# Hybrid attention and mLSTM layer: four kinds of TensorE transpose moved to the DMA crossbar, and one score product per chunk

## The reference, cut to what matters

```python
h = rmsnorm(x, norm_g)
aq, ak, av, az, mq, mk, mv, mo, mz, gates = split(h @ w_in)      # 6672 columns
# group A: 8 query heads, 2 key/value heads, head width 128
aq, ak = rope(rmsnorm(aq)), rope(rmsnorm(ak))
attn = softmax(aq @ ak.T / sqrt(128)) @ av * silu(az)
# group B: mLSTM, 4 heads, q/k width 128, v width 256, chunks of 128 tokens,
# one scan forward and one backward over the same q, k, v with their own gates:
qk  = (q @ k.T) * w                    # w: lower (forward) or upper (backward) triangle with decays
num = qk @ v + si * (q @ C);  den = sum(qk) + si * (q @ n);  hd = num / max(|den|, exp(-m))
C   = sc * C + (we * k).T @ v          # n likewise
hm  = rmsnorm(sigmoid(mo) * (h_fwd + h_bwd)) * silu(mz)
y   = x + concat(attn, hm) @ w_out
```

## Time and profile before

| what | us |
|---|---|
| median of 6 runs (lowest, highest) | 4178.82 (3975.4, 4428.89) |
| the profiled execution | 3974.4 |
| its span on the slowest core (core 4) | 3973.4 |
| spans of the 8 cores | 3956.2 to 3973.4 |
| TensorE matmul busy | 3871.7 |
| VectorE, ScalarE, GpSimd busy | 1791.8, 1640.4, 1036.0 |

### The profile page before, as it was taken

One profiled execution on the slowest core, in us unless ns is written; L12 is line 12 of the kernel. 1 busy time (PEld: TensorE's weight loads), 2 busy tenths in 40 slices (PEclk: granted clock), 3 DMA queues, 4 the chain that ended last, 5 costly groups with the idle time before them and its releaser, 6 DMA issues.

```text
span 3973.4 us, 97401 instructions; the slowest of 8 cores (3956.2 to 3973.4 us)
## 1 busy us (share of the span) xinstructions
PE 3871.7 (97%) x36966; PEld 3192.4 (80%) x36966; DVE 1791.8 (45%) x5039; ACT 1640.4 (41%) x3373; POOL 1036.0 (26%) x1907
## 2 busy tenths in 40 slices
PE   6999999999989999999999998999999999999999
PEld 5778776887878887887687787888878767778888
DVE  5444342555733344334255574334334425556522
ACT  5665762323332256666332333224665643333200
POOL 5244131222310144234022231005314402223200
PEclk9999999999999999999999999999999999999999
DMA  7321211121268611111111215762111111211364
GB/s 203 66 44 28 40 27 33 23 44 33 58 174 237 189 44 40 24 39 35 33 23 33 44 34 166 237 203 62 27 32 41 39 22 23 44 35 26 81 193 148
DMA packets 78220, 290.59 MB, mean 73 GB/s; under 512 B 8640, under 2 KB 33600, under 8 KB 58560
## 3 DMA queue, kind: packets, MB, share of 16 engines
q0 software_dynamic: 14832, 107.03, 14.9%
q1 hardware_dynamic: 62928, 177.33, 13.5%
HBM read 341.01 MB, written 50.33 MB: 98 GB/s over the span
## 4 chain that ended last, share of the span: by engine, by line
PE 90%; DMA 4%; ACT 2%; issue 1%; DVE 1%; POOL 1%; SPq 0%; DVEq 0%; ACTq 0%; POOLq 0%
PE PP L930 15%; PE PP L791 8%; PE PP L807 8%; PE PP L808 8%; PE PP L782 8%; PE PP L685 8%; PE PP L731 8%; PE PP L632 7%; PE PP L698 7%; PE PP L634 4%; DMA arena<-xr 3%; PE PP L855 2%; PE PP L839 1%; PE PP L547 1%; DVE mixT L694 1%
## 5 line engine op out<-in xcount | busy, mean ns | idle before, releaser
L930 PE MATMUL PP<-WR,mixT 128*128 128x256 bf16 x6144 | 686.7, 275 | 27.1 <-DVE arena L931 27.1
L930 PEld LDWEIGHTS PP<-WR,mixT 128*128 128x128 bf16 x6144 | 603.4, 99 | 102.5 <-issue 29.3
L729 ACT ACTIVATE arena<-PP 128x1024 bf16<-128x1024 f32 x576 | 570.9, 1023 | 159.5 <-PE PP L698 156.0
L698 PE MATMUL PP<-mixT 128*128 128x512 bf16 x1536 | 454.2, 378 | 6.9 <-ACT mixT L729 6.9
L685 PE MATMUL PP<-WR,hT 128*128 128x256 bf16 x3072 | 417.6, 274 | 18.8 <-DVE mixT L694 15.4
L807 PE MATMUL PP<-WR,hT 128*128 128x256 bf16 x3072 | 398.6, 273 | 0.0
L685 PEld LDWEIGHTS PP<-WR,hT 128*128 128x128 bf16 x3072 | 292.5, 98 | 131.2 <-issue 43.2
L515 POOL DMA_DIRECT2D WR<-wt x102 | 62.4, 612 | 1262.8 <-PE PP L731 728.6
L859 POOL TENSOR_TENSOR arena<-arena,g_lam 128x257 bf16<-128x257 f32 x360 | 230.0, 655 | 600.5 <-PE PP L828 365.7
L632 PE MATMUL PP<-WR,hT 128*128 128x256 bf16 x3072 | 370.4, 273 | 4.0 <-DVE hT L549 4.0
L931 DVE TENSOR_TENSOR arena<-PP,arena 128x256 f32<-128x256 f32 x384 | 158.2, 423 | 478.5 <-PE PP L930 403.7
(11 more groups left out here) (110 smaller groups left out, 5100.5 us busy)
## 6 DMA issues: line engine op xcount, KB each, us to landing
WR<-wt POOLq DMA_DIRECT2D x102, 1024.0 KB, 10.3
arena<-xr SPq DMA_DIRECT2D x96, 512.0 KB, 6.2
y<-arena SPq DMA_DIRECT2D x96, 512.0 KB, 3.8
arena<-x SPq DMA_DIRECT2D x32, 1024.0 KB, 7.1
arena<-c_rope SPq DMA_DIRECT2D x192, 128.0 KB, 2.0
mixT<-x SPq DMA_DIRECT2D x16, 1024.0 KB, 6.7
arena<-c_f SPq DMA_DIRECT2D x3, 256.0 KB, 4.1
csm<-c_sm SPq DMA_DIRECT2D x1, 212.0 KB, 14.1
```

The lines of the kernel that those rows point to most:

```text
L698: S.group('pe', [(P.matmul, (sp_[:, 512 * u:512 * (u + 1)], kT[:, (2 * j + u) * 128:(2 * j + u + 1) * 128], qT[:, n % 2, qsl(n)]), dict(st ...
L729: S.op('act', A.activation, PT[j], spair[j % 2][:, 0:1024], AF.Exp, scale=128.0 ** 0.5)
L930: S.mm(pb, [(mixT[:, kc, T * 128:(T + 1) * 128], WO[:, kc, :]) for kc in range(KC)])
```

## The change

Queries and keys, attention output, mLSTM output and mLSTM keys are transposed by `dma_start_transpose`, issued on SyncE's queue (`S.turn`), from SBUF to SBUF. `proj_xpose` and `out_xpose` and the evictions behind them are gone. The transposes of `fin` write mixT without the norm weights; when four tiles of a group are done, VectorE multiplies the 512 columns in place. Keys are transposed once per head, 512 tokens at a time, into `ktm`. The score product of a chunk is made once, at steps i below 8, and masked for both directions at once into 24 slots `Pm`. The last `step_dC` of a head, whose result nothing reads, is dropped. PSUM banks that become free go to the gate path (two banks in turn) and to the mLSTM's projections (three in turn instead of two). The arena grows by 12160 bytes per partition, out of a smaller scratch of GpSimd's DMAs. `out_proj` takes the groups q in the order 1, 2, 0, 3, and the planner models two DMA queues that share the bandwidth.

```diff
+    def turn(self, out, in_, sem):
+        return self._add('sp', [(self.nc.sync.dma_start_transpose, (), dict(out=out, in_=in_))], dma=sem,
+                         line=sys._getframe(1).f_lineno)
...
-                dma_free = max(dma_free, s) + op.nbytes / 330.0
-                done = max(s + 2000.0, dma_free + 1700.0)
+                done = self.dma_done(q_free, e, s, op.nbytes)
...
-ARENA_BYTES = 42752
+ARENA_BYTES = 54912
+NPM = 24
...
-    nc = bass.Bass("TRN2", target_bir_lowering=False)
+    nc = bass.Bass("TRN2", target_bir_lowering=False, dynamic_dma_scratch_size=4096)
...
+        qkT = carve_hi(0, [128, 3, SEQ], BF16)
-        RA = 4
+        RA, RQ = 4, 6
-        qr = [carve(5376 * r + 4608, [128, 3, 128], BF16) for r in range(RA)]
+        qr = [carve(42752 + 768 * r, [128, 384], BF16) for r in range(RQ)]
...
-        def proj_xpose(T, nh):
...
-            S.group('pe', [(P.transpose, (ptr[:, h, :], qr[b][:, h, :], identb), {}) for h in range(nh)])
-            S.op('dve', V.tensor_copy, qT[:, :, T * 128:(T + 1) * 128], ptr[:, 0:2, :])
-            if nh == 3:
-                S.op('dve', V.tensor_copy, kT[:, T * 128:(T + 1) * 128], ptr[:, 2, :])
+            S.turn(qkT[:, 0:nh, Ts], qb[:, 0:128 * nh], 'tq%d' % (T % RQ))
...
-        pz = bank(3)
+        pz = [bank(3), bank(2)]
...
-            def out_xpose(n):
-                o = ob[n % 2]
-                S.group('pe', [(P.transpose, (ptr_o[:, 128 * t:128 * (t + 1)], o[:, t, :], identb), {}) for t in range(4)])
-                S.op('dve', V.tensor_copy, mixT[:, 2 * p + n % 2, qsl(n)], ptr_o)
+                S.turn(mixT[:, 2 * p + n % 2, qsl(n)].rearrange("p (t e) -> p t e", t=4), o, 'to%d' % (n % 2))
...
-                return bank(2 + cnt['f'] % 2)
+                return bank((0, 2, 3)[cnt['f'] % 3])
...
                     S.op('dve', V.tensor_copy, km[h][:, ts], pb)
+                    S.turn(ktm[h % 2][:, 4 * tb:4 * tb + 4, :], km[h][:, ts], 'tk%d' % (4 * (h % 2) + tb))
...
-                S.group('pe', [(P.transpose, (otr[:, k, :], ob[:, k * 128:(k + 1) * 128], identb), {}) for k in range(2)])
-                S.op('dve', V.tensor_tensor, mixT[:, 8 + 2 * h:10 + 2 * h, Ts], otr,
-                     gmcol[:, 2 * h:2 * h + 2].unsqueeze(2).to_broadcast([128, 2, 128]), ALU.mult)
+                S.turn(mixT[:, 8 + 2 * h:10 + 2 * h, Ts], ob, 'tf%d' % bo)
+                fdone[(h, T // 4)] = fdone.get((h, T // 4), 0) + 1
+                if fdone[(h, T // 4)] == 4:
+                    for k in range(8 + 2 * h, 10 + 2 * h):
+                        m = mixT[:, k, (T // 4) * 512:(T // 4 + 1) * 512]
+                        S.op('dve', V.tensor_scalar, m, m, gmcol[:, k - 8:k - 7], None, ALU.mult)
...
-                S.group('pe', [(P.transpose, (ktr[dr], km[h][:, csl(i, dr)], identb), {}) for dr in range(2)])
-                S.group('pe', [(P.matmul, (sm[dr], km[h][:, csl(i, dr)], qm[h][:, csl(i, dr)]), dict(start=True, stop=True))
-                               for dr in range(2)])
-                for dr in range(2):
+                if i < NT // 2:
+                    S.group('pe', [(P.matmul, (sm[dr], km[h][:, csl(i, dr)], qm[h][:, csl(i, dr)]), dict(start=True, stop=True))
+                                   for dr in range(2)])
+                for dr in range(2 if i + 1 < NT else 0):
...
-                    step_dC(h, i)
+                    if i + 1 < NT:
+                        step_dC(h, i)
...
-                for q in range(4):
-                    r = q % 2
+                for n_, q in enumerate((1, 2, 0, 3)):
+                    r = n_ % 2
```

More of the change, by code:

```diff
@@ L234, in dma, with dma_done @@
         return op
+    def turn(self, out, in_, sem):
+        return self._add('sp', [(self.nc.sync.dma_start_transpose, (), dict(out=out, in_=in_))], dma=sem,
+                         line=sys._getframe(1).f_lineno)
+    @staticmethod
+    def dma_done(q_free, e, s, nbytes):
+        o = 'pool' if e == 'sp' else 'sp'
+        t, b = nbytes / 330.0, max(q_free[e], s)
+        both = min(2 * t, max(q_free[o] - b, 0.0))
+        q_free[e] = b + t + both / 2
+        if both:
+            q_free[o] += both / 2
+        return max(s + 2000.0, q_free[e] + 1700.0)
     def schedule(self):
@@ L246, in schedule @@
         avail = {e: [] for e in engs}
-        dma_free = port = 0.0
+        port = 0.0
+        q_free = {'sp': 0.0, 'pool': 0.0}
         for op in ops:
@@ L616, in build_program @@
         oc = carve(40192, [128, 4, 129], F32)
-        ob = [carve_hi(29760 + 1024 * r, [128, 4, 128], BF16) for r in range(2)]
-        RA = 4
+        ob = [carve_hi(29760 + 1024 * r, [128, 512], BF16) for r in range(2)]
+        RA, RQ = 4, 6
         xg = [carve(5376 * r, [128, 3, 128], F32) for r in range(RA)]
@@ L656, in proj_tile @@
             S.op('dve', V.tensor_tensor, t1[b][:, 0:nh, :], t1[b][:, 0:nh, :], t2[b][:, 0:nh, :], ALU.add)
-            S.op('pool', G.tensor_tensor, qr[b][:, 0:nh, :], t1[b][:, 0:nh, :],
+            qb = qr[T % RQ]
+            S.op('pool', G.tensor_tensor, qb.rearrange("p (h e) -> p h e", h=3)[:, 0:nh, :], t1[b][:, 0:nh, :],
                  st[:, c_rs:c_rs + nh].unsqueeze(2).to_broadcast([128, nh, 128]), ALU.mult)
-        def proj_xpose(T, nh):
-            b = T % RA
-            ptr = bank16(2)[:, 0:384].rearrange("p (h e) -> p h e", h=3)
-            S.group('pe', [(P.transpose, (ptr[:, h, :], qr[b][:, h, :], identb), {}) for h in range(nh)])
-            S.op('dve', V.tensor_copy, qT[:, :, T * 128:(T + 1) * 128], ptr[:, 0:2, :])
-            if nh == 3:
-                S.op('dve', V.tensor_copy, kT[:, T * 128:(T + 1) * 128], ptr[:, 2, :])
+            S.turn(qkT[:, 0:nh, Ts], qb[:, 0:128 * nh], 'tq%d' % (T % RQ))
         NJ = NT // 2
@@ L683, in zmm @@
                 m, half = (u % 8) // 2, part // 4
+                pz_ = pz[u % 2]
                 T = 4 * m + 2 * (u % 2) + half
-                S.group('pe', [(P.matmul, (pz[:, 256 * half:256 * (half + 1)], hT[:, kc, T * 128:(T + 1) * 128], WZ[:, kc, :]),
+                S.group('pe', [(P.matmul, (pz_[:, 256 * half:256 * (half + 1)], hT[:, kc, T * 128:(T + 1) * 128], WZ[:, kc, :]),
                                 dict(start=(kc == 0), stop=(kc == KC - 1)))
@@ L692, in sig @@
                 sz = zg[(u // 2) % 2][:, 2 * (u % 2):2 * (u % 2) + 2, :].rearrange("p a b -> p (a b)")
-                S.op('act', A.activation, sge, pz, AF.Tanh, scale=0.5)
-                S.op('dve', V.scalar_tensor_tensor, sz, sge, 1.0, pz, ALU.add, ALU.mult)
+                S.op('act', A.activation, sge, pz[u % 2], AF.Tanh, scale=0.5)
+                S.op('dve', V.scalar_tensor_tensor, sz, sge, 1.0, pz[u % 2], ALU.add, ALU.mult)
             def s_pair(n, j):
@@ L706, in epilogue @@
                 for t in range(4):
-                    S.op('dve', V.scalar_tensor_tensor, o[:, t, :], oc[:, t, 0:128], r[:, t:t + 1],
+                    S.op('dve', V.scalar_tensor_tensor, o[:, 128 * t:128 * t + 128], oc[:, t, 0:128], r[:, t:t + 1],
                          z[:, t, 128 * (n % 2):128 * (n % 2) + 128], ALU.mult, ALU.mult)
-            def out_xpose(n):
-                o = ob[n % 2]
-                S.group('pe', [(P.transpose, (ptr_o[:, 128 * t:128 * (t + 1)], o[:, t, :], identb), {}) for t in range(4)])
-                S.op('dve', V.tensor_copy, mixT[:, 2 * p + n % 2, qsl(n)], ptr_o)
+                S.turn(mixT[:, 2 * p + n % 2, qsl(n)].rearrange("p (t e) -> p t e", t=4), o, 'to%d' % (n % 2))
             if p == 0:
@@ L737, in attention @@
                         sig(u + 1)
-                    if j == 3 and n > 0:
-                        out_xpose(n - 1)
                     S.bias = 60
@@ L743, in attention @@
                 epilogue(n)
-            out_xpose(7)
         vext = carve(0, [128, NT, VS], BF16)
@@ L749, in build_program @@
         Cs = [carve(28960 + 528 * d_, [128, 264], BF16) for d_ in range(2)]
[L750 to L753, removed]
+        kx = [[carve(30016 + 256 * (3 * d_ + r), [128, 128], BF16) for r in range(3)] for d_ in range(2)]
+        sozb = [carve(31552 + 2048 * r, [128, 512], F32) for r in range(3)]
+        obb = [carve(37696 + 512 * r, [128, 256], BF16) for r in range(4)]
+        ktm = [carve(39744 + 4096 * r, [128, NT, 128], BF16) for r in range(2)]
+        Pm = [carve(47936 + 256 * r, [128, 128], BF16) for r in range(NPM)]
         qm = [mixT[:, 8 + 2 * h_, :] for h_ in range(4)]
@@ L757, in mlstm @@
         def mlstm():
-            ktr = [bank16(0)[:, 128 * d_:128 * (d_ + 1)] for d_ in range(2)]
             sm = [bank(1)[:, 128 * d_:128 * (d_ + 1)] for d_ in range(2)]
-            otr = bank16(1)[:, 512:768].rearrange("p (k e) -> p k e", k=2)
             pN = [bank(6 + d_)[:, 0:257] for d_ in range(2)]
@@ L766, in mlstm @@
             hfree = list(range(NHS))
+            pslot = {}
+            pfree = list(range(NPM))
             W = {}
+            fdone = {}
             def w_head(h, tag):
@@ L802, in fin @@
```

(33 more changed lines are left out.)

1 line of the change is left out of this document (removed).

## The result

The changed kernel takes 4064.24 us (median of 10 runs) against 3978.65 us (median of 20 runs of the kernel before): a ratio of 1.0214, 95% interval 1.0203 to 1.0225. It is slower by 2.1%; the forecast was 3876 us, 2.5% faster.

What follows compares the result with a forecast made beforehand. The prediction took TensorE, busy 3871.7 of 3973.4 us, as the bound: 3974.4 - 103.0 (instructions removed) - 8 (second gate bank) + 13 (lost in projections) = 3876 us, 2.5% faster, range 3832 to 4000.

Steps and rivals of the forecast that it cites:

- At 0.5 to 1.0 us a block nothing of it reaches the path: 0 us: Crossbar transposes in projections, attention and mLSTM: claimed hidden behind each stage's work, adding 0 us.
- the keys' cover: Start of attention after an even projection: latest keys are read 9.3 us in, covering a landing of 2 us.
- What TensorE gives back, 55 ns a transpose: Transposes and half the scores leaving TensorE: each gives back its distance to the next start, 55 ns.
- The sum of 98 us: Whole kernel: 103.0 us off TensorE plus 8 for the gate bank, less 13 taken back in the projections.
- The second bank, 8 us: Gate path: a second PSUM bank removes 8 of 15.4 us in which TensorE waits for the only bank's reading.
- The crossbar's own rate, under 1.0 us a block: SyncE's queue: a 128x128 transpose taken at 0.5 to 1.0 us, from the rope table's 2.0 us landing.
- Rival B: Crossbar at 2.1 us a block delays keys before attention: about 4080 us, break-even 1.73 us a block, chance 0.17.
- The scaling, 0 us: mLSTM output, VectorE's norm-weight multiplication: its wait is covered to 3.5 us beyond 2 us; 10.3 us landings would cost 230.
- The keys, 0 us: Attention after an even projection: transposed keys land within 9.3 us of cover, so no wait.
- The residual, 0 us between -27 and +27: Turn from mLSTM to output projection: residual loads queue behind the last transposes; the 27.1 us wait counted as unchanged.

Runs made afterwards that it cites:

- all3: Changed kernel with weight loads held for an even projection's last transpose, norm-weight scaling three tiles later, gate path on one PSUM bank: 3904.97 us, 0.9821 of the kernel before.
- defer: Changed kernel with only the scaling by the norm weights recorded three tiles later: 3979.6 and 3986.9 us.
- hold: Changed kernel with only the weight loads recorded behind an even projection made to wait for its last transpose: 1.0047 of the kernel before, 3996.3 us at the lowest.

## Why the prediction was wrong

The direction was wrong, and one step made it so: "At 0.5 to 1.0 us a block nothing of it reaches the path: 0 us". I had the right place twice and the right size once. I wrote that the keys' cover is for "a landing of 2 us", and that a landing of 10.3 us, as of a weight load, would cost 230 us at the scaling. I then took the landing of about 2 us everywhere; the latest took 24.2 us. What I did not ask is what else starts at that moment. The end of a projection frees two weight buffers, and in the case shown their loads go out within 2 us of the last keys (418.50, 420.21, 420.33). In five of the six even groups a load was still in flight when the last keys were issued, and these are the 5 waits of L708; in the sixth the loads had gone out 14 us before (2803.58 and 2817.22), and nothing waits. The mLSTM has the same meeting when its weights change.

- **What TensorE gives back, 55 ns a transpose: right.** In the kernel before, a step of the mLSTM with one tile takes 7.98 us (timeline):

```profile
863.77 3.66 PE L791 MATMUL PP<-WR,hT 128*128 128x256 bf16 x32
871.75 3.66 PE L791 MATMUL PP<-WR,hT 128*128 128x256 bf16 x32
```

  and in the kernel after 7.65 us:

```profile
720.85 3.66 PE L797 MATMUL PP<-WR,hT 128*128 128x256 bf16 x32
728.50 3.66 PE L797 MATMUL PP<-WR,hT 128*128 128x256 bf16 x32
```

  0.33 us for four transposes and two scores, 55 ns each.
- **The sum of 98 us: right in size where nothing is late.** With 4 weight loads the change gains 85.7 us. Part of the rest may be waiting for exponentials: L737 and L708 wait 31 us for L735 in the kernel after, against 9 us in the one before.
- **The second bank, 8 us: consistent** with all3, not resolved.
- **The crossbar's own rate, under 1.0 us a block: not contradicted, and not what decides.** Keys, 4 blocks, land in 2.6 us at the median, two or three blocks of queries and keys in 2.3. Rival B fell with its 2.1 us a block; that its 4078 us is close to the measured 4064 is chance. (Its break-even comes to 1.74 us a block, not 1.73.) The Trainium skill puts a block at 1309 ns ("VectorE: DVE Perf Modes", The three transpose paths). By that, as an estimate, four blocks would take 5.2 us; the measured 2.6 us is half of it.
- **The scaling, 0 us: wrong**, 191.3 us in 41 waits of VectorE, of which 55.0 us appear as TensorE's waits for the state update, and about 81 us in the time that `defer` takes off.
- **The keys, 0 us: wrong**, 44.2 us in 5 waits; 68 us with what `hold` takes off. The price of the clock is in neither step: I had none for it, and it is the 49 us of the same matmuls above.
- **The residual, 0 us between -27 and +27: inside its ends**, 40.6 us instead of 27.1.

## What to carry to other kernels

When a transfer takes the place of an engine's work, don't price it by its median landing: list which other transfers start at the same moment, above all the prefetch that the same end of a stage sets free. Then either hold the prefetch back or put distance between the landing and the first in-order reader; here these two edits turned 2.1% slower into 2.0% faster, and smaller prefetch packets made it 2.6%. And a wait of TensorE costs more than its length: here 154 us of idle time came with 49 us of slower matmuls.

## What was not expected of the hardware

- Issuing a transpose occupies SyncE's queue for 1.17 to 1.19 us at the median, against 0.33 us for a rope table in the kernel before.
- While two DMA queues had work, their packets went one for one whatever their size (50 and 49 in 2 us), so that one queue had 97.5% of the engines' time and the other 4.6%.
- After 11.09 us without a matmul the same matmuls ran at half speed (1.87 us for four of L708 instead of 1.03), that is at 1.2 instead of 2.4 GHz, and the clock was back at 1.00 in the window from 460 on.
- Weight loads cost the kernel with the crossbar 217 us and the one without 46 us, at the same bytes.
